# Attention probabilities: the multiply by the reciprocal moves from VectorE to ScalarE in every second head

## The chip, the cores and the metric

The kernel runs on one core of a Trainium2 chip. Its time is the device time of one execution in microseconds (us); before the change it is 2204.34 us, the median of 3 runs (2202.94 to 2204.92). The engines named below are TensorE (PE, with its weight loads PEld), VectorE (DVE), ScalarE (ACT), GpSimd (POOL) and SyncE (SP). Each engine runs its own list of instructions in order and waits at semaphores for the others.

## The reference

One layer of a hybrid encoder for 1024 prompt rows and 64 sample rows: projections, a retention branch with four heads, an attention branch (MLA) with eight heads, gates, an output projection and a SwiGLU stage. The part that matters here is the softmax of the attention:

```python
def mla_attend(q, k_nope, kpe, v, mask):
    scale = (NOPE_DIM + ROPE_DIM) ** -0.5
    s = (jnp.einsum('bqhd,bkhd->bhqk', q[..., :NOPE_DIM], k_nope).astype(jnp.float32)
         + jnp.einsum('bqhr,bkr->bhqk', q[..., NOPE_DIM:], kpe).astype(jnp.float32)) * scale
    s = jnp.where(mask, s, jnp.finfo(jnp.float32).min)
    p = jax.nn.softmax(s, axis=-1)
    return jnp.einsum('bhqk,bkhe->bqhe', p.astype(v.dtype), v)
```

Queries of tile t (128 rows) see keys 0 to 128(t+1); the 64 sample rows see 320 keys.

## The kernel before

The eight attention heads run one after another. A head h has nine tiles in the order 8, 0, 1, ..., 7: tile 8 is the sample rows (64 x 320 scores), tile t has 128 x 128(t+1). A function, `attention_steps(head)`, writes out nine steps per head as a list, and all five engines walk the same list, each doing its own share of every entry. Step k of a head holds, in this order:

- P of tile k+1: the probabilities are normalised. VectorE takes the reciprocal of the row sum (L1875) and multiplies the exponentials `p_exp` in place (L1876); this raises `prob_done`. In a head's last step this is tile 8 of the next head.
- T of tile k: TensorE transposes the probabilities in blocks of up to 512 keys into PSUM (L980, after `prob_done` and after VectorE has emptied the bank); ScalarE copies each block out rounded, `pt_hi` (L1355); VectorE subtracts to get the remainder, `pt_lo` (L1640).
- O of a pair of tiles, in some steps: probabilities times values on TensorE, then `out_hl` high on ScalarE (L1368) and low on VectorE. O also needs a free PSUM bank: the unit two places before it must have been emptied by VectorE (`p_free`).
- D, in the steps after one that made a rotary part: ScalarE copies the rotated query parts to `qr` (L1296, L1297), VectorE subtracts (L1640).
- S of tile k+2: scores on TensorE (L800 to L967), the row maximum on VectorE (L1868, L1869), the exponential with its row sum on ScalarE (L1340).
- F: one to three projection units for the next head, as filling for TensorE: K, Q and V (copied high on ScalarE at L1272, L1283, L1277, low on VectorE). While an odd head (1, 3, 5) runs, three units more belong to the list, R: the rotary query parts of the next two heads. VectorE multiplies these by cosine and sine (L1684 and four pieces of L1675, all on VectorE), GpSimd adds the products (L2206), and D of the next step stores them. In head 7 the filling is the first retention projection, whose inputs are loaded again from DRAM.

`p_exp`, `negmax` and `rowsum` have two buffers each, by the parity of the tile's running number n.

In the texts below the steps of an odd head are called by the P that they begin with: t0 to t7 for its tiles 0 to 7, and "the sample step" for the last step of the even head before it, which holds P of the odd head's tile 8.

Of the kernel before, what the change touches and what calls it, by code (L numbers as in the profile page):

```python
# [8 lines left out]
ACT = mybir.ActivationFunctionType  # L9
AX = mybir.AxisListType  # L10

P = 128
# [124 lines left out]
def keys_of(tile):  # L137

    return (0, (tile + 1) * P, P) if tile < 8 else (SEQ, DEC + PAST, DEC)


def build(nc, a, o):

    with ExitStack() as ctx:
# [5 lines left out]
        def sem(name):  # L150
            return ctx.enter_context(nc.semaphore(name))
# [14 lines left out]
        rowsum = at("rowsum", CON + 1344, [2, 2])  # L166
# [44 lines left out]
        p_exp = [region(f"p_exp{b}", 23.7, [SEQ], extra=4096 * b) for b in range(2)]  # L211
# [131 lines left out]
        max_done = sem("max_done")  # L343
        exp_done = sem("exp_done")
        prob_done = sem("prob_done")
        t_done = sem("t_done")
        t_high = sem("t_high")
        t_low = sem("t_low")
# [68 lines left out]
        def s_index(h, tile):  # L417
            return 9 * h + (0 if tile == 8 else tile + 1)
# [751 lines left out]
        def _(act):  # L1170
# [43 lines left out]
            for t in range(KT):  # L1214
                act.wait_ge(x_in[t], 16)
                nc.scalar.activation(xa_hi[:, t, :], xt[:, t, :], ACT.Copy,
                                     scale=gains[:, G_MIX + t:G_MIX + t + 1]).then_inc(norm_high, 1)
# [106 lines left out]
            for head in range(MH):  # L1324
                for s in attention_steps(head):
                    if s[0] == "F":
                        fill(*s[1:])
                        continue
                    h, tile = s[1:]
                    if s[0] == "D":  # L1330
                        rotary_parts(*s[1:])
                    elif s[0] == "S":
                        n = s_index(h, tile)
                        _, nk, nq = keys_of(tile)
                        act.wait_ge(max_done, n + 1)
                        if n >= 2:
                            act.wait_ge(t_done, t_end(n - 2))
                        bank = 2 * (n % 2)
                        src = ps[0:nq, bank:bank + 2, :].rearrange("p b k -> p (b k)")[:, 0:nk]
                        nc.scalar.activation(p_exp[n % 2][0:nq, 0:nk], src, ACT.Exp,  # L1340
                                             bias=negmax[0:nq, n % 2, 0:1], scale=SCALE,
                                             accum_out=rowsum[0:nq, n % 2, 0:1]).then_inc(exp_done, 1)
                    elif s[0] == "T":
                        _, nk, nq = keys_of(tile)
                        q0 = P * (tile % 2) if tile < 8 else P
                        for i, (k0, nb) in enumerate(t_blocks(tile)):
                            t = t_index(h, tile) + i
                            act.wait_ge(t_done, t + 1)
                            if i == 0 and (tile % 2 == 0) and (h or tile != 8):

                                act.wait_ge(p_done, 1 + (p_order["M", h - 1, "O", 3] if tile == 8 else
                                                     p_order["M", h, "O", tile // 2 - 1 if tile else 4]))
                            full = nb if tile < 8 else 2
                            src = ps[:, 4 + t % 2, 0:full * P].rearrange("p (k q) -> p k q", k=full)[:, :, 0:nq]
                            ins = nc.scalar.activation(pt_hi[:, k0:k0 + full, q0:q0 + nq], src, ACT.Copy)  # L1355
                            if tile == 8:
                                ins = nc.scalar.activation(pt_hi[0:DEC, 2, q0:q0 + nq],
                                                           ps[0:DEC, 4 + t % 2, 2 * P:2 * P + nq], ACT.Copy)
                            ins.then_inc(t_high, 1)
                    elif s[0] == "O":  # L1360
                        pair = s[2]
                        n = o_index(h, pair)
                        w = DEC if pair == 4 else 2 * P
                        u = p_order["M", h, "O", pair]
                        act.wait_ge(p_done, u + 1)
                        if n >= 2:
                            act.wait_ge(o_out[n % 2], 16 * (n // 2))
                        nc.scalar.activation(out_hl[n % 2][:, 0, 0:w], ps[:, 6 + u % 2, 0:w],  # L1368
                                             ACT.Copy).then_inc(p_high, 1)


            for h in range(RH):
                for s in retention_steps(h):
# [4 lines left out]
                    n = 9 * h + c  # L1378
                    L = P if c < 8 else DEC
                    if s[0] == "A":  # L1380
                        col = 1 if c < 8 else 2
                        act.wait_ge(kd_done, n + 1)
                        if n >= 2:
                            act.wait_ge(u_done, n - 1)
                        nc.scalar.activation(kd_f[n % 2][0:L, :], ps[0:L, 3, 0:DK], ACT.Copy,
                                             scale=dcol[0:L, h, col:col + 1]).then_inc(kd_copy, 1)
                    elif s[0] == "B":
                        act.wait_ge(z_done, n + 1)
                        if n >= 2:
                            act.wait_ge(z_norm, n - 1)  # L1390
                        nc.scalar.activation(zs[n % 2][0:L, :], ps[0:L, 1, 0:DV], ACT.Copy,
                                             scale=dcol[0:L, h, 0:1]).then_inc(z_copy, 1)
                    elif s[0] == "Z":
# [3 lines left out]
                        for j in range(2):  # L1397
                            ins = nc.scalar.activation(zt[n % 2][:, j, 0:L], ps[:, 2, j * P:j * P + L], ACT.Copy,
                                                       scale=gains[:, G_GN + 2 * h + j:G_GN + 2 * h + j + 1])
# [69 lines left out]
            for s, t in enumerate(OUT_ORDER):  # L1469
                for g, (c0, c1) in enumerate(GROUPS):  # L1470
                    q = 3 * s + g
                    w = c1 - c0
                    if g == 0:
# [3 lines left out]
                        else:  # L1477
# [3 lines left out]
                                         scale=gains[:, G_F + t:G_F + t + 1]).then_inc(h_gain, 1)  # L1481
# [48 lines left out]
            for pair in range(UP_PAIRS):  # L1530
                n = pair + 1
# [84 lines left out]
        def _(dve):  # L1616
            chained = [0]

            def chain(ins):

                chained[0] += 1
                ins.then_inc(v_chain, 1)
                dve.wait_ge(v_chain, chained[0])
# [227 lines left out]
            for head in range(MH):  # L1851
                for s in attention_steps(head):
                    if s[0] == "F":
                        fill(*s[1:])
                        continue
                    h, tile = s[1:]
                    if s[0] == "D":
                        rotary_parts(*s[1:])
                    elif s[0] == "S":
                        n = s_index(h, tile)  # L1860
                        _, nk, nq = keys_of(tile)
                        bank = 2 * (n % 2)
                        scores = ps[0:nq, bank:bank + 2, :].rearrange("p b k -> p (b k)")
                        dve.wait_ge(s_done, n + 1)
                        if tile < 8:

                            chain(nc.vector.memset(scores[0:64, nk - 64:nk], NEG))
                        chain(nc.vector.reduce_max(negmax[0:nq, n % 2, 1:2], scores[:, 0:nk], AX.X))  # L1868
                        nc.vector.tensor_scalar(negmax[0:nq, n % 2, 0:1], negmax[0:nq, n % 2, 1:2],  # L1869
                                                -SCALE, None, ALU.mult).then_inc(max_done, 1)  # L1870
                    elif s[0] == "P":
                        n = s_index(h, tile)
                        _, nk, nq = keys_of(tile)
                        dve.wait_ge(exp_done, n + 1)
                        chain(nc.vector.reciprocal(rowsum[0:nq, n % 2, 1:2], rowsum[0:nq, n % 2, 0:1]))  # L1875
                        nc.vector.tensor_scalar(p_exp[n % 2][0:nq, 0:nk], p_exp[n % 2][0:nq, 0:nk],  # L1876
                                                rowsum[0:nq, n % 2, 1:2], None, ALU.mult).then_inc(prob_done, 1)
                    elif s[0] == "T":
                        n = s_index(h, tile)
                        _, nk, nq = keys_of(tile)  # L1880
                        q0 = P * (tile % 2) if tile < 8 else P
                        for i, (k0, nb) in enumerate(t_blocks(tile)):
                            t = t_index(h, tile) + i
                            dve.wait_ge(t_high, t + 1)
                            full = nb if tile < 8 else 2
                            src = ps[:, 4 + t % 2, 0:full * P].rearrange("p (k q) -> p k q", k=full)[:, :, 0:nq]
                            ins = low(pt_lo[:, k0:k0 + full, q0:q0 + nq], src, pt_hi[:, k0:k0 + full, q0:q0 + nq])
                            if tile == 8:
                                ins = low(pt_lo[0:DEC, 2, q0:q0 + nq], ps[0:DEC, 4 + t % 2, 2 * P:2 * P + nq],
                                          pt_hi[0:DEC, 2, q0:q0 + nq])  # L1890
                            ins.then_inc(t_low, 1)
                    elif s[0] == "O":
                        pair = s[2]
                        n = o_index(h, pair)
                        w = DEC if pair == 4 else 2 * P
                        u = p_order["M", h, "O", pair]
                        dve.wait_ge(p_high, high_index["M", h, "O", pair] + 1)
                        low(out_hl[n % 2][:, 1, 0:w], ps[:, 6 + u % 2, 0:w],
                            out_hl[n % 2][:, 0, 0:w]).then_inc(p_free, 1)
# [157 lines left out]
            for pair in range(UP_PAIRS):  # L2057
                n = pair + 1
# [387 lines left out]
```

## Time and profile before

| | |
|---|---|
| median of 3 runs | 2204.34 us |
| profiled execution | 2203.62 us, its span 2201.7 us |
| mean granted TensorE clock | 0.972 of full speed |
| busy: PE / PEld / DVE / ACT / POOL | 94% / 90% / 49% / 30% / 16% |
| attention heads | 164 to 582 us of the span |

In the tenths of the span that the page gives (40 slices of 55 us) the attention fills slices 4 to 11, and VectorE shows 7 to 4 tenths there, TensorE 8 and 9:

```profile
PE   7879898987998988999999999988999999999997
DVE  7966767764444433321111224475555556432257
ACT  4434444441112223321121113354434334310010
PEclk9989999998999999999999999999999999999998
```

A line such as `247.68 1.19 DVE L1876 TENSOR_SCALAR p_exp<-p_exp,rowsum 128x896 ... x1` in the trace is: start in the span, duration, engine, line of the kernel, operation, what is written from what, the tile's shape and how many are merged. Square brackets behind it give how long the engine was idle before, and who released it.

### The profile page before, as it was taken

To read this page: it belongs to the slowest core of one execution; us is meant where nothing else is said; L and a number is where in the kernel's file an instruction comes from. 1 tells how busy PE (TensorE), PEld (TensorE's weight loads), DVE (VectorE), ACT (ScalarE), POOL (GpSimd) and SP (SyncE) were. 2 spreads that over 40 slices of the span, in tenths; PEclk is the share of its full clock that TensorE was granted. 3 is DMA by queue.
4 is the path that set the end of the run, shared out by engine and by line. 5 is a ranking of instruction groups with operands and counts; after the bars stand their busy time and mean duration, and the time that the engine had idled before them with its cause. 6 is when DMAs were issued, how large, how long until landed. Compare 5 with 4: busy or idle time off the path is not lost. (4 is left out here: it accounts for less than half of the span.)

```text
span 2201.7 us, 33255 instructions
## 1 busy us (share of the span) xinstructions
PE 2062.5 (94%) x13370; PEld 1979.3 (90%) x13370; DVE 1086.7 (49%) x1820; ACT 662.3 (30%) x1191; POOL 348.9 (16%) x307
## 2 busy tenths in 40 slices
PE   7879898987998988999999999988999999999997
PEld 6768787876998887999999999988999999999997
DVE  7966767764444433321111224475555556432257
ACT  4434444441112223321121113354434334310010
POOL 2110000000122111000000000144444444300000
PEclk9989999998999999999999999999999999999998
DMA  3511110115111112221124112423233232473412
GB/s 146 217 45 41 40 45 31 45 35 212 59 33 59 41 42 72 82 67 42 48 91 158 38 48 79 132 76 119 90 109 115 85 118 98 165 297 137 165 58 82
DMA packets 88842, 201.60 MB, mean 92 GB/s; under 512 B 11664, under 2 KB 42320, under 8 KB 85904
## 3 DMA queue, kind: packets, MB, share of 16 engines
q1 hardware_dynamic: 88720, 199.89, 26.3%
q8 instruction: 86, 1.41, 0.3%
q14 instruction: 36, 0.29, 0.0%
HBM read 141.71 MB, written 58.15 MB: 91 GB/s over the span
## 5 line engine op out<-in xcount | busy, mean ns | idle before, releaser
L800 PE MATMUL ps<-xn_hi,w_hi 128*128 128x384 f32 (+1 forms) x960 | 320.6, 334 | 20.4 <-DMA xn_lo<-xn_spill 12.6
L800 PE MATMUL ps<-sx_hi,t_hi 128*128 128x272 f32 x1056 | 306.3, 290 | 12.1 <-ACT u L1495 5.9
L802 PE MATMUL ps<-xn_lo,w_hi 128*128 128x384 f32 (+1 forms) x960 | 317.5, 331 | 0.0
L801 PE MATMUL ps<-xn_hi,w_lo 128*128 128x384 f32 (+1 forms) x960 | 317.5, 331 | 0.0
L801 PE MATMUL ps<-sx_hi,t_lo 128*128 128x272 f32 x1056 | 306.0, 290 | 0.0
L802 PE MATMUL ps<-sx_lo,t_hi 128*128 128x272 f32 x1056 | 304.8, 289 | 0.0
L800 PEld LDWEIGHTS ps<-sx_hi,t_hi 128*128 128x128 f32 x1056 | 200.8, 190 | 13.1 <-issue 6.9
L800 PEld LDWEIGHTS ps<-xn_hi,w_hi 128*128 128x128 f32 x960 | 183.9, 192 | 24.5 <-DMA xn_lo<-xn_spill 15.7
L801 PEld LDWEIGHTS ps<-sx_hi,t_lo 128*128 128x128 f32 x1056 | 200.5, 190 | 0.1
L802 PEld LDWEIGHTS ps<-sx_lo,t_hi 128*128 128x128 f32 x1056 | 200.5, 190 | 0.0
L801 PEld LDWEIGHTS ps<-xn_hi,w_lo 128*128 128x128 f32 x960 | 183.9, 192 | 0.0
L802 PEld LDWEIGHTS ps<-xn_lo,w_hi 128*128 128x128 f32 x960 | 183.7, 191 | 0.0
L1628 DVE TENSOR_TENSOR w_lo<-w_stage,w_hi 128x1024 fp32r<-128x1024 f32 (+1 forms) x83 | 98.4, 1185 | 121.7 <-ACT w_hi L1177 121.4
L1177 ACT ACTIVATE w_hi<-w_stage 128x1024 fp32r<-128x1024 f32 (+1 forms) x83 | 84.2, 1015 | 156.8 <-PE ps L802 142.9
L800 PE MATMUL ps<-y_hi,w_hi 128*128 128x384 f32 (+1 forms) x384 | 126.3, 329 | 3.8 <-DMA y_lo<-ym_spill 3.8
L802 PE MATMUL ps<-y_lo,w_hi 128*128 128x384 f32 (+1 forms) x384 | 126.2, 329 | 0.0
L801 PE MATMUL ps<-y_hi,w_lo 128*128 128x384 f32 (+1 forms) x384 | 126.1, 328 | 0.0
L2129 DVE TENSOR_TENSOR hacc<-hacc,ps 128x384 f32<-128x384 f32 (+3 forms) x96 | 51.0, 532 | 140.3 <-PE ps L802 140.2
L802 PE MATMUL ps<-yd,dwr_hi 128*128 128x384 f32 (+3 forms) x324 | 105.8, 326 | 0.0
L801 PE MATMUL ps<-yd,dwr_lo 128*128 128x384 f32 (+3 forms) x324 | 105.7, 326 | 0.0
L800 PE MATMUL ps<-yd,dwr_hi 128*128 128x384 f32 (+3 forms) x324 | 105.6, 326 | 0.0
L1340 ACT ACTIVATE p_exp<-ps,negmax 64x320 f32<-64x320 f32 (+8 forms) x72 | 51.7, 718 | 162.2 <-DVE negmax L1869 162.1
(245 smaller groups left out, 4757.3 us busy)
## 6 DMA issues: line engine op xcount, KB each, us to landing
w_stage<-in_weights SPq DMA_DIRECT2D x83, 512.0 KB, 3.7
y_spill<-hg_r SPq DMA_DIRECT2D x44, 544.0 KB, 3.3
yd<-y_spill SPq DMA_DIRECT2D x22, 1088.0 KB, 5.6
raw<-in_weights SPq DMA_DIRECT2D x22, 512.0 KB, 5.1
hg<-in_weights SPq DMA_DIRECT2D x22, 512.0 KB, 5.1
d_stage<-in_weights SPq DMA_DIRECT2D x24, 384.0 KB, 3.1
ym_spill<-out_hl SPq DMA_DIRECT2D x32, 256.0 KB, 2.6
xt<-in_x SPq DMA_DIRECT2D x8, 544.0 KB, 8.1
```

The source lines that it names most:

```text
L800: nc.tensor.matmul(out, wh, xh, start=start, stop=False, skip_group_check=onto)
L801: nc.tensor.matmul(out, wl, xh, start=False, stop=False, skip_group_check=onto)
L802: return nc.tensor.matmul(out, wh, xl, start=False, stop=stop, skip_group_check=onto)
L1177: nc.scalar.activation(w_hi[:, slot, first:8, :], stage[slot][:, first:8, :], ACT.Copy).then_inc(w_high, 1)
L1340: nc.scalar.activation(p_exp[n % 2][0:nq, 0:nk], src, ACT.Exp, bias=negmax[0:nq, n % 2, 0:1], scale=SCALE, accum_out=rowsum[0:nq, n % 2, 0 ...
L1628: nc.vector.tensor_tensor(w_lo[:, slot, first:8, :], stage[slot][:, first:8, :], w_hi[:, slot, first:8, :].bitcast(F32), ALU.subtract).the ...
L2129: nc.vector.tensor_tensor(hacc[:, t, c0:c1], hacc[:, t, c0:c1], ps[:, bank, 0:c1 - c0], ALU.add).then_inc(d_free, 1)
```

## The change

In the heads with an odd number, 36 of the 72 P entries, VectorE only makes the reciprocal and raises a new semaphore, `sum_inv`. ScalarE gets the P entry: it waits for `sum_inv` and multiplies `p_exp` in place with an ACTIVATE whose scale is the per-row reciprocal; it raises `prob_done`. In the even heads nothing changes.

```diff
@@ ScalarE's list
                     elif s[0] == "S":
...
+                    elif s[0] == "P" and h % 2:
+                        n = s_index(h, tile)
+                        _, nk, nq = keys_of(tile)
+                        act.wait_ge(sum_inv, 9 * (h // 2) + n - 9 * h + 1)
+                        nc.scalar.activation(p_exp[n % 2][0:nq, 0:nk], p_exp[n % 2][0:nq, 0:nk], ACT.Copy,
+                                             scale=rowsum[0:nq, n % 2, 1:2]).then_inc(prob_done, 1)
                     elif s[0] == "T":
@@ VectorE's list
                         dve.wait_ge(exp_done, n + 1)
+                        if h % 2:
+                            nc.vector.reciprocal(rowsum[0:nq, n % 2, 1:2], rowsum[0:nq, n % 2, 0:1])\
+                              .then_inc(sum_inv, 1)
+                            continue
                         chain(nc.vector.reciprocal(rowsum[0:nq, n % 2, 1:2], rowsum[0:nq, n % 2, 0:1]))
                         nc.vector.tensor_scalar(p_exp[n % 2][0:nq, 0:nk], p_exp[n % 2][0:nq, 0:nk],
                                                 rowsum[0:nq, n % 2, 1:2], None, ALU.mult).then_inc(prob_done, 1)
```

ScalarE's list in head 1, from the exponential of tile 6 (896 keys) to that of tile 7, before the change (line numbers of the kernel before):

```order
L1340 ACTIVATE p_exp_105,rowsum<-ps,negmax 128x896 [waits t_done,max_done]
L1355 ACTIVATE pt_hi<-ps 128x4x128 [waits t_done]
L1355 ACTIVATE pt_hi<-ps 128x2x128 [waits t_done]
L1296 ACTIVATE qr_111<-tmp_56 64x320 [waits rot_sum]
L1297 ACTIVATE qr_112<-tmp_56 64x320
L1340 ACTIVATE p_exp_106,rowsum<-ps,negmax 128x1024 [waits t_done,max_done]
```

The same place after the change (line numbers of the changed kernel, 1 to 7 higher):

```order
L1341 ACTIVATE p_exp_105,rowsum<-ps,negmax 128x896 [waits t_done,max_done]
L1348 ACTIVATE p_exp_105<-p_exp_105,rowsum 128x896 [waits sum_inv]
L1362 ACTIVATE pt_hi<-ps 128x4x128 [waits t_done]
L1362 ACTIVATE pt_hi<-ps 128x2x128 [waits t_done]
L1297 ACTIVATE qr_111<-tmp_56 64x320 [waits rot_sum]
L1298 ACTIVATE qr_112<-tmp_56 64x320
L1341 ACTIVATE p_exp_106,rowsum<-ps,negmax 128x1024 [waits t_done,max_done]
```

The multiply of tile 6, with its wait for VectorE, now stands ahead of the copies of tile 5's transposed blocks and of the rotary copies.

VectorE's list at the same place, from the last rotation to the next row maximum, before:

```order
L1684 TENSOR_TENSOR tmp_54<-ps,cos_91 128x320 [waits rot_sum,p_done]
L1675 TENSOR_TENSOR tmp_55<-ps,sin_92 32x320 x4
L1875 RECIPROCAL rowsum<-rowsum 128x1 [waits exp_done]
L1876 TENSOR_SCALAR p_exp_105<-p_exp_105,rowsum 128x896 [waits v_chain]
L1640 TENSOR_TENSOR pt_lo<-ps,pt_hi 128x4x128 [waits t_high]
L1640 TENSOR_TENSOR pt_lo<-ps,pt_hi 128x2x128 [waits t_high]
L1640 TENSOR_TENSOR qr_113<-tmp_56,qr_113 64x320 [waits rot_high]
```

And after:

```order
L1883 RECIPROCAL rowsum<-rowsum 128x1 [waits exp_done]
L1647 TENSOR_TENSOR pt_lo<-ps,pt_hi 128x4x128 [waits t_high]
L1647 TENSOR_TENSOR pt_lo<-ps,pt_hi 128x2x128 [waits t_high]
L1647 TENSOR_TENSOR qr_113<-tmp_56,qr_113 64x320 [waits rot_high]
L1647 TENSOR_TENSOR qr_114<-tmp_56,qr_114 64x320
```

The multiply is gone, and what now stands behind the reciprocal waits for a copy that ScalarE makes behind its own multiply.

## Rows read from the trace of the kernel before

**Rows 1.** Two windows: length, busy PE, PEld, DVE, ACT, POOL, granted clock, DMA.

```profile
202.82:257.82 55.00, 48.23 (x308) 42.14 (x306) 41.39 (x95) 21.62 (x55) 3.87 (x5) 1.00 0.13 40
...
340.00:350.00 10.00, 7.28 (x43) 6.71 (x42) 9.12 (x18) 3.29 (x7) 0.86 (x1) 0.85 0.08 26
```

**Rows 2.** Timeline of TensorE: start, duration, operation, idle before it and its releaser.

```profile
205.86 0.36 PE L980 MATMUL ps<-eye,p_exp 64*128 64x64 f32 x3 [0.41 <-DVE pt_lo L1640]
...
222.87 0.36 PE L800 MATMUL ps<-pt_hi,v_hi 128*128 128x256 f32 x1
...
260.86 0.36 PE L980 MATMUL ps<-eye,p_exp 64*128 64x64 f32 x3 [0.80 <-DVE pt_lo L1640]
...
513.57 0.45 PE L800 MATMUL ps<-xn_hi,w_hi 128*128 128x384 f32 x1 [3.62 <-DMA xn_lo<-xn_spill]
```

**Rows 3.** Timeline of VectorE, sample step, then t1 and t2 of head 1.

```profile
204.56 0.15 DVE L1875 RECIPROCAL rowsum<-rowsum 64x1 f32<-64x1 f32 x1
...
205.04 1.27 DVE L1640 TENSOR_TENSOR pt_lo<-ps,pt_hi 128x512 fp32r<-128x512 f32 x2
...
215.22 0.15 DVE L1875 RECIPROCAL rowsum<-rowsum 128x1 f32<-128x1 f32 x1
...
215.68 0.28 DVE L1640 TENSOR_TENSOR pt_lo<-ps,pt_hi 128x128 fp32r<-128x128 f32 x1
...
218.70 0.15 DVE L1875 RECIPROCAL rowsum<-rowsum 128x1 f32<-128x1 f32 x1
...
219.23 0.42 DVE L1640 TENSOR_TENSOR pt_lo<-ps,pt_hi 128x256 fp32r<-128x256 f32 x1
...
221.90 0.56 DVE L1640 TENSOR_TENSOR q_lo<-ps,q_hi 128x384 fp32r<-128x384 f32 x1 [1.23 <-ACT q_hi L1283]
```

**Rows 4.** Timeline of VectorE and GpSimd in t4, t6 and t7 of head 1.

```profile
232.33 0.16 DVE L1875 RECIPROCAL rowsum<-rowsum 128x1 f32<-128x1 f32 x1
...
234.51 1.12 DVE L1640 TENSOR_TENSOR qr<-tmp,qr 64x384 fp32r<-64x384 f32 x2
...
247.48 0.17 DVE L1875 RECIPROCAL rowsum<-rowsum 128x1 f32<-128x1 f32 x1
247.53 0.86 POOL L2206 TENSOR_TENSOR tmp<-tmp,tmp 128x320 f32<-128x320 f32 x1 [6.75 <-DVE tmp L1675]
247.68 1.19 DVE L1876 TENSOR_SCALAR p_exp<-p_exp,rowsum 128x896 f32<-128x896 f32 x1
...
249.95 0.99 DVE L1640 TENSOR_TENSOR qr<-tmp,qr 64x320 fp32r<-64x320 f32 x2
...
254.88 0.15 DVE L1875 RECIPROCAL rowsum<-rowsum 128x1 f32<-128x1 f32 x1
...
255.07 0.75 DVE L1876 TENSOR_SCALAR p_exp<-p_exp,rowsum 128x1024 f32<-128x1024 f32 x1
255.73 1.15 DVE L1640 TENSOR_TENSOR pt_lo<-ps,pt_hi 128x512 fp32r<-128x512 f32 x2
```

**Rows 5.** Timeline of VectorE and ScalarE, between t6 and t7.

```profile
252.36 0.15 DVE L1869 TENSOR_SCALAR negmax<-negmax 128x1 f32<-128x1 f32 x1
252.55 1.11 ACT L1340 ACTIVATE p_exp<-ps,negmax 128x1024 f32<-128x1024 f32 x1 [3.18 <-DVE negmax L1869]
...
253.65 0.59 ACT L1277 ACTIVATE v_hi<-ps 128x512 fp32r<-128x512 f32 x1
254.13 0.98 ACT L1355 ACTIVATE pt_hi<-ps 128x512 fp32r<-128x512 f32 x2
254.27 0.69 DVE L1640 TENSOR_TENSOR v_lo<-ps,v_hi 128x512 fp32r<-128x512 f32 x1 [1.76 <-ACT v_hi L1277]
```

**Rows 6.** Groups by form on ScalarE: count, then busy us and mean ns.

```profile
L1340 ACT ACTIVATE p_exp<-ps,negmax 128x512 f32<-128x512 f32 x8 | 5.5, 689 | 17.9 <-DVE negmax L1869 17.9
...
L1296 ACT ACTIVATE qr<-tmp 64x384 fp32r<-64x384 f32 x6 | 3.2, 526 | 14.5 <-POOL tmp L2206 14.5
...
L1216 ACT ACTIVATE xa_hi<-xt,gains 128x1088 fp32r<-128x1088 f32 x8 | 9.6, 1202 | 1.5 <-DMA xt<-in_x 1.2
```

More of the change, by code:

```diff
@@ L345, in build @@
         prob_done = sem("prob_done")
+        sum_inv = sem("sum_inv")
         t_done = sem("t_done")
```

## The prediction

> **What bounds the kernel now.** I read the page first: TensorE is busy 94% of the span, so only a place where TensorE waits can carry a change on another engine. Then the windows, a row per head: in the 55.00 us of head 1 TensorE is busy 48.23, so it waits 6.8 us, although VectorE, at 41.39 us, has room on average [rows 1]. Then the timelines of TensorE and VectorE side by side. TensorE waits at the joint of heads 0 and 1 for `pt_lo` (0.41 us) and again at the joint of 1 and 2 (0.80 us) [rows 2]. Traced back from the second joint, VectorE runs without a gap from the first rotation to the row maximum before t7, and from there VectorE and ScalarE take turns: maximum, exponential, `v_hi`, `v_lo`, reciprocal, multiply, `pt_lo`, maximum. The reader is to see the turns in [rows 5]: ScalarE starts 0.04 us after VectorE's 252.51 end, VectorE 0.03 us after ScalarE's 254.24, and neither does anything else useful in between. From the sample step to the first rotation (some 24 us) TensorE sets the pace. So VectorE's chain is the path from the first rotation of an odd head to the start of the next head, and in the sample step. Heads 1, 3 and 5 have this pattern; head 7 has not.
>
> **What the change does in one step.** Before: reciprocal, multiply, `pt_lo` at once, because ScalarE had copied `pt_hi` meanwhile. After: reciprocal; 0.04 us to ScalarE; the multiply there, A; the copy of the first block of `pt_hi`, H, which starts 0.10 us before A's end (254.13 against 253.65 + 0.59 [rows 5]); 0.03 us back. From the start of the reciprocal to `pt_lo` that is 0.15 + 0.04 + A - 0.10 + H + 0.03 = A + H + 0.12. ScalarE is free when the reciprocal comes, since its exponential is long done.
>
> Prices. H: the 512-wide copy of PSUM takes 0.59 us [rows 5]. The slope of ScalarE is (1.11 - 0.689) / 512, 0.053 us per 64 elements [rows 5, 6]; so H is 0.38 at 256 wide and 0.27 at 128. A is not in the trace; the nearest row has the same shape of operation, SBUF to SBUF with a per-row scale: 1.202 us at 1088 elements [rows 6]. By the slope A is 1.15 at 1024, 1.04 at 896, 0.83 at 640, 0.62 at 384, 0.57 at 320, 0.52 at 256. It could be as low as an exponential without its pointer, some 0.1 less each, or as high as one without the 0.10 overlap; I take the row, and keep both ends.
>
> **Step by step**, new interval less old:
>
> - Sample step (320 wide, 512-wide block): 0.57 + 0.59 + 0.12 = 1.28 against 0.48 (204.56 to 205.04 [rows 3]): +0.80. TensorE waits for this `pt_lo` already [rows 2], so all of it counts.
> - t0: `pt_lo` waits for TensorE, not for the multiply: nothing.
> - t1: 0.52 + 0.27 + 0.12 = 0.91 against 0.46: +0.45. t2: 0.62 + 0.38 + 0.12 = 1.12 against 0.53: +0.59 [rows 3]. TensorE sets the pace here and needs neither `pt_lo` at once. But both delay the exponential behind which ScalarE copies `q_hi`, and so `q_lo`, which ended at 222.46 [rows 3], by 0.80 + 0.45 + 0.59 = 1.84, to 224.30. O of the first pair needs the bank that `q_lo` frees. It began at 222.87 [rows 2]; now 224.30 + 0.06 for the hand-over. So TensorE is 1.49 late there, not 0.80: a new wait of 0.69 us. t3 is absorbed: VectorE waits for TensorE's scores behind it.
> - t4, t5, t6, the rotary steps, with VectorE on the path: here `pt_lo` itself is hardly later (the multiply it loses took 1.19 us at 896 wide [rows 4]), but the copies of the rotary part stand behind on ScalarE. t4, reciprocal to `qr` low: 0.16 + 0.04 + 0.83 - 0.10 + 0.49 (a 512-wide block less the overlap) + 2 x 0.53 + 0.03 = 2.51 against 2.18 (232.33 to 234.51): +0.33. t6: 0.16 + 0.04 + 1.04 - 0.10 + 0.77 (0.49 and 0.28, two blocks) + 2 x 0.47 + 0.03 = 2.88 against 2.47: +0.41 [rows 4, 6]. (The second `qr` size by the same slope.) t5 lies between, 0.37. Together +1.11.
> - t7: 1.15 + 0.59 + 0.12 = 1.86 against 0.85 (254.88 to 255.73 [rows 4]): +1.01. Its cover, that ScalarE copies early, is gone, and the turns of VectorE and ScalarE are the path.
> - The last P of an odd head belongs to an even head: unchanged. In the even head every engine starts later by the same amount, and TensorE sets the pace, so nothing is won back.
>
> An odd head costs 1.49 + 1.11 + 1.01 = 3.61 us with its sample step. Three of them: 10.8. Head 7 adds only its sample step, 0.80: this delays the last O of head 6, whose emptied bank lets the input loads start, and TensorE then waits for these (3.62 us at 513.57 [rows 2]). Behind them its steps are long retention projections without waits, so P of head 7 is hidden. Sum: +11.6 us. The profiled execution took 2203.62 us; 2203.62 + 11.6 = 2215.2. The median of the runs is 0.72 above the profiled one: 2216.
>
> Behind the attention TensorE works almost without waits, so I let the delay pass to the end undiminished.
>
> **Two rules weighed.** In t6 the multiply on VectorE took 1.19 us for 896 elements while GpSimd added (247.53 to 248.39); in t7, where GpSimd does nothing, 0.75 for 1024 [rows 4]. The Trainium skill, "SBUF — State Buffer", section "Who interferes with whom", has it that VectorE and GpSimd share a port pair that one holds for a whole instruction, and that ScalarE has its own. The trace agrees; by that rule alone the move would pay in t4 to t6. Against it stands the Trainium skill, "ScalarE: Activation LUTs", section "Rules for kernel authors", which wants a plain multiply on VectorE; and its section on the table load gives 186 ns plus 0.833 ns per element plus 93 ns for a pointer, an estimate of 1.13 us at 1024, with which the sum would be some 0.4 us less. No run so far shows this very instruction.
>
> **Rivals.**
>
> 1. *Covered multiply, faster.* Place: t4 to t7. VectorE loses 1.19 us three times and 0.75 once per odd head, 4.3 us, and if ScalarE's copies did not follow its multiply, VectorE would be early by this: 3 x 4.3 = 13 us, 2204.3 - 13 = 2191. For it: VectorE really is without a gap there. Against: the order of ScalarE's list. It decides from A + H + 0.12 below the old interval; in t6 A would have to be about 0.7 instead of 1.04 for `pt_lo`, and lower for `qr`. 7 in 100.
> 2. *Hidden, no change.* The waits at the joints would have to have room; they are all put down to VectorE. Within 0.2%, 2200 to 2208.8: 6 in 100.
> 3. *No wait at the O bank.* If `q_lo` does not hold it, a head costs 0.80 + 1.11 + 1.01 = 2.92; 3 x 2.92 + 0.80 = +9.6, 2214. With the low end of A besides, 0.4 to 0.5 less per head: +8, 2212. 20 in 100 for up to 2213.
> 4. *The clock.* In head 3, with the gaps of TensorE as in head 1, the granted clock fell to 0.85 in 10 us, part of it at 1.2 instead of 2.4 GHz [rows 1]; there it cost nearly nothing, since VectorE was the path. Wider gaps could bring it in each odd head and where TensorE is the path: 10 x 0.15 = 1.5 us each, +4.5 on my sum, 2220. 10 in 100.
>
> **Numbers.** My own case, 2213 to 2218.5 (the high end is 0.10 without overlap in seven steps of each head, +2.1), has 57 in 100. The range goes from 2209 to 2220: it leaves out the first two rivals and the far end of the fourth. 0.2%, 4.4 us, is about what a measurement of this kernel can tell from no change. Faster 0.07, same 0.06, slower 0.87.
>
> **What would show it.** Right: in the odd heads ScalarE's new line takes 0.83 us at 640 and 1.15 at 1024; VectorE has a new idle time before `pt_lo`, released by `pt_hi`, of some 1 to 1.5 us in t1 to t7; TensorE has a new wait of about 0.7 us before O of the first pair; the joints of the heads move: 205.86 to 260.86, 55.0 us, becomes 57.8, and the even head after it is 0.8 us longer by its sample step, and behind 582 us nothing moves. Wrong: if VectorE's maxima of t5 to t7 come earlier than before relative to the joint, the first rival holds; if the joints are as far apart as before, the second.

## The result and the profile after

The changed kernel takes 2215.52 us, the median of 4 runs (2214.13 to 2218.94), against 2203.72 us for the kernel before (4 runs, 2202.94 to 2204.92): ratio 1.0055, 95% interval 1.0038 to 1.0073, slower by 11.8 us. 2216 was predicted. The single executions scatter by several us (4.8 us among the four of the changed kernel), so that the median fell within 0.5 us of the forecast is partly luck; what follows goes by the profiled pair. The profiled execution took 2214.64 us against 2203.62, +11.02, with a span of 2212.7; its mean granted clock is 0.972 as before.

The page's busy line of the changed kernel: VectorE gives up 24 us (1086.7 before), ScalarE takes 24 (662.3 before), TensorE's share falls since the span grows.

```profile
PE 2061.9 (93%) x13370; PEld 1979.2 (89%) x13370; DVE 1062.9 (48%) x1784; ACT 686.2 (31%) x1227; POOL 348.1 (16%) x307
```

The timeline of TensorE, changed kernel, at the places of [rows 2]. A "joint" here is the start of the three merged transposes of a head's sample tile, where one head ends and the next begins. First the joint of heads 0 and 1, then O of the first pair, then the transposes of tile 6, then the joint of heads 1 and 2:

```profile
206.89 0.36 PE L981 MATMUL ps<-eye,p_exp 64*128 64x64 f32 x3 [1.19 <-DVE pt_lo L1647]
...
224.61 0.36 PE L801 MATMUL ps<-pt_hi,v_hi 128*128 128x256 f32 x1 [0.49 <-issue]
...
252.37 1.72 PE L981 MATMUL ps<-eye,p_exp 128*128 128x128 f32 x7 [3.18 <-DVE pt_lo L1647]
...
264.55 0.36 PE L981 MATMUL ps<-eye,p_exp 64*128 64x64 f32 x3 [1.17 <-DVE pt_lo L1647]
```

ScalarE's exponential ahead of the first of these joints, kernel before, then changed kernel:

```profile
202.82 0.52 ACT L1340 ACTIVATE p_exp<-ps,negmax 64x320 f32<-64x320 f32 x1 [1.47 <-DVE negmax L1869]
```

```profile
203.07 0.52 ACT L1341 ACTIVATE p_exp<-ps,negmax 64x320 f32<-64x320 f32 x1 [1.47 <-DVE negmax L1876]
```

This execution was already 0.25 us late at the exponential ahead of the joint (203.07 against 202.82). The wait at the first joint grew from 0.41 to 1.19 us, by 0.78. O has a new wait, for which the trace names no releaser (`issue`); the next timeline shows whom it fits. From joint to joint head 1 takes 264.55 - 206.89 = 57.66 us instead of 55.00, and head 2, to the joint at 307.20, 42.65 instead of 41.80.

The timeline of VectorE, changed kernel, in the sample step, t1, t2, t4, t6 and t7, answers to [rows 3] and [rows 4]:

```profile
204.80 0.14 DVE L1883 RECIPROCAL rowsum<-rowsum 64x1 f32<-64x1 f32 x1
206.06 1.29 DVE L1647 TENSOR_TENSOR pt_lo<-ps,pt_hi 128x512 fp32r<-128x512 f32 x2 [1.11 <-ACT pt_hi L1362]
...
217.13 0.29 DVE L1647 TENSOR_TENSOR pt_lo<-ps,pt_hi 128x128 fp32r<-128x128 f32 x1 [0.74 <-ACT pt_hi L1362]
...
221.27 0.42 DVE L1647 TENSOR_TENSOR pt_lo<-ps,pt_hi 128x256 fp32r<-128x256 f32 x1 [0.95 <-ACT pt_hi L1362]
...
223.95 1.02 DVE L1647 TENSOR_TENSOR q_lo<-ps,q_hi 128x384 fp32r<-128x384 f32 x2 [1.23 <-ACT q_hi L1284]
...
234.06 0.16 DVE L1883 RECIPROCAL rowsum<-rowsum 128x1 f32<-128x1 f32 x1
...
236.55 1.12 DVE L1647 TENSOR_TENSOR qr<-tmp,qr 64x384 fp32r<-64x384 f32 x2 [0.25 <-ACT qr L1298]
...
249.78 0.16 DVE L1883 RECIPROCAL rowsum<-rowsum 128x1 f32<-128x1 f32 x1
251.53 1.02 DVE L1647 TENSOR_TENSOR pt_lo<-ps,pt_hi 128x512 fp32r<-128x512 f32 x2 [1.59 <-ACT pt_hi L1362]
252.64 0.98 DVE L1647 TENSOR_TENSOR qr<-tmp,qr 64x320 fp32r<-64x320 f32 x2
...
257.56 0.15 DVE L1883 RECIPROCAL rowsum<-rowsum 128x1 f32<-128x1 f32 x1
259.41 1.16 DVE L1647 TENSOR_TENSOR pt_lo<-ps,pt_hi 128x512 fp32r<-128x512 f32 x2 [1.70 <-ACT pt_hi L1362]
```

In every step shown `pt_lo` has a wait that it did not have before, 0.74 us in t1 to 1.70 in t7, and its releaser is `pt_hi`. The `q_lo` at 223.95 is two merged blocks; the first of them, at the 0.56 us that one takes in [rows 3], ends at 224.51, and O starts 0.10 us behind it, at 224.61. Ahead of `pt_hi` stands ScalarE's own new instruction; groups by form, changed kernel, of the attention:

```profile
L1348 ACT ACTIVATE p_exp<-p_exp,rowsum 128x1024 f32<-128x1024 f32 x4 | 4.6, 1150 | 6.6 <-DVE rowsum L1883 6.6
...
L1348 ACT ACTIVATE p_exp<-p_exp,rowsum 128x640 f32<-128x640 f32 x4 | 3.3, 833 | 15.4 <-DVE rowsum L1883 15.4
```

### The profile page after: what moved, and what is told of

Read it like the earlier page. It is cut to its first block and busy times, and to the rows that moved or that the text cites. A ratio compares the mean times of both kernels' runs of the same rounds, so it can differ in the third digit from the quotient of the medians.

```text
span 2212.7 us, 33255 instructions
## 1 busy us (share of the span) xinstructions
PE 2061.9 (93%) x13370; PEld 1979.2 (89%) x13370; DVE 1062.9 (48%) x1784; ACT 686.2 (31%) x1227; POOL 348.1 (16%) x307
## 5 line engine op out<-in xcount | busy, mean ns | idle before, releaser
L801 PEld LDWEIGHTS ps<-sx_hi,t_hi 128*128 128x128 f32 x1056 | 200.8, 190 | 13.1 <-issue 6.9
```

Of the source, the lines that this page charges most:

```text
L801: nc.tensor.matmul(out, wh, xh, start=start, stop=False, skip_group_check=onto)
```

## The experiments

Single medians turned out to scatter by more than some effects here, so the parts are read by the joints, which stand once per head in TensorE's timeline. Before, head 1 takes 55.00 us from joint to joint [rows 2], head 2 41.80, head 3 55.16 and head 5 55.00.

**Four parts of the change.** Each moves only some of the multiplies; `moved` is the list of their running numbers.

```diff
-                    elif s[0] == "P" and h % 2:
+                    elif s[0] == "P" and on_act(h, tile):
...
-                        act.wait_ge(sum_inv, 9 * (h // 2) + n - 9 * h + 1)
+                        act.wait_ge(sum_inv, moved.index(n) + 1)
...
-                        if h % 2:
+                        if on_act(h, tile):
```

with `on_act` true in odd heads for tile 8 (part_sample), tiles 0 to 3 (part_t0_t3), 4 to 6 (part_t4_t6), or 7 (part_t7).

> Only the sample tile's multiply (320 keys) of heads 1, 3, 5 and 7 goes to ScalarE, 4 of the 36 moved ones; the rest stays on VectorE. Theory (the multiply stands in series ahead of the pt_hi copy that VectorE waits for): the joint ahead of each odd head comes 0.78 us later and TensorE's wait there grows from 0.41 to about 1.2 us; three heads and head 7: +3.1 us in all; inside the odd head nothing moves (205.9 to 260.9 stays 55.0 us). Rival by busy time (the cost follows the time that ScalarE gains): 4 x 0.56 of the 26 us moved, so 9% of 11 us, +1 us. Rival that only the rotary steps count: 0.

> Only the multiplies of tiles 0 to 3 in the odd heads go to ScalarE, 16 of 36. Theory: VectorE is 0.45 + 0.59 = 1.04 us later at q_lo of the first Q unit, and O of the first pair waits for the bank that it frees: 0.7 us more per head of 1, 3 and 5, seen as a new idle time of TensorE of some 0.5 us or more before O, and nothing behind it; +2.1 us in all. Rival by busy time: 16 x 0.56 of 26 us, +3.8 us. Rival (TensorE sets the pace here, all is hidden): 0.

> Only the multiplies of tiles 4 to 6 in the odd heads go to ScalarE, 12 of 36. Theory: the multiply that VectorE loses is as long as what it waits for, but the qr copies stand behind: +0.31, +0.27, +0.39 us from reciprocal to the low part of qr, 0.97 per head of 1, 3 and 5, so +2.9 us; in head 7 nothing. Rival by busy time: 12 x 0.94 of 26 us, +4.8 us. Rival that the freed VectorE time (1.2 us each) is worth something here when nothing else is changed: below 0.

> Only the multiply of tile 7 (1024 keys) in the odd heads goes to ScalarE, 4 of 36. Theory: reciprocal to pt_lo goes from 0.85 to 1.85 us, all of it on the path at the end of heads 1, 3 and 5: +3.0 us; in head 7 nothing. Rival by busy time: 4 x 1.15 of 26 us, +1.9 us. Rival that TensorE hides it: 0.

The first and the last line of each fence are the two joints of head 1 in TensorE's timeline; in part_t0_t3 the O stands between them. part_sample:

```profile
206.76 0.36 PE L986 MATMUL ps<-eye,p_exp 64*128 64x64 f32 x3 [1.19 <-DVE pt_lo L1652]
...
261.74 0.36 PE L986 MATMUL ps<-eye,p_exp 64*128 64x64 f32 x3 [0.80 <-DVE pt_lo L1652]
```

part_t0_t3:

```profile
207.86 0.36 PE L986 MATMUL ps<-eye,p_exp 64*128 64x64 f32 x3 [0.41 <-DVE pt_lo L1652]
225.59 0.35 PE L806 MATMUL ps<-pt_hi,v_hi 128*128 128x256 f32 x1 [0.50 <-issue]
...
263.58 0.36 PE L986 MATMUL ps<-eye,p_exp 64*128 64x64 f32 x3 [0.79 <-DVE pt_lo L1652]
```

part_t4_t6:

```profile
207.32 0.36 PE L986 MATMUL ps<-eye,p_exp 64*128 64x64 f32 x3 [0.40 <-DVE pt_lo L1652]
...
263.25 0.36 PE L986 MATMUL ps<-eye,p_exp 64*128 64x64 f32 x3 [0.79 <-DVE pt_lo L1652]
```

part_t7:

```profile
207.88 0.36 PE L986 MATMUL ps<-eye,p_exp 64*128 64x64 f32 x3 [0.40 <-DVE pt_lo L1652]
...
263.86 0.36 PE L986 MATMUL ps<-eye,p_exp 64*128 64x64 f32 x3 [1.16 <-DVE pt_lo L1652]
```

| kernel | time in us, ratio to before (95%) | head 1, joint to joint | more | expected |
|---|---|---|---|---|
| part_sample | 2207.35, 1.0016 (1.0005 to 1.0028) | 54.98 | 0; the wait ahead of it +0.78 | 0; +0.78 |
| part_t0_t3 | 2207.99, 1.0017 (1.0005 to 1.0028) | 55.72 | +0.72 | +0.7 |
| part_t4_t6 | 2207.51, 1.0014 (1.0002 to 1.0025) | 55.93 | +0.93 | +0.97 |
| part_t7 | 2208.68, 1.0018 (1.0006 to 1.0029) | 55.98 | +0.98 | +1.0 |
| the change | 2215.52, 1.0055 (1.0038 to 1.0073) | 57.66 | +2.66 | +2.8 |

The three inner parts sum to 2.63 us, the whole gives 2.66: they are independent links of one path. By the rival of busy time the four would have been 1, 3.8, 4.8 and 1.9 us; by the joints they are 4 x 0.78 = 3.1, 3 x 0.72 = 2.2, 3 x 0.93 = 2.8 and 3 x 0.98 = 2.9, together 11.0. The medians alone would not decide this: the four parts are 2.7, 3.4, 2.9 and 4.1 us above the kernel before as measured beside them (2204.62), together 13.1, each with an interval of some 2.5 us to either side. The waits stand where each part says: 1.19 us at the joint for the sample, 0.50 at O for t0 to t3, 1.16 at the far joint for t7. No rival that hides one of them is left.

**The place in the list: late_odd, late_all.** The multiply on ScalarE moves behind the copies of the transposed blocks: in late_odd the multiplies of the odd heads, as in the change, in late_all those of all heads but the very first tile. ScalarE's list, against the kernel before; `scaled_late` is the wait and the ACTIVATE of the change.

```diff
+                    elif s[0] == "P" and on_act(h, tile):
+                        pending = (h, tile)
...
                             ins.then_inc(t_high, 1)
+                        if pending is not None:
+                            scaled_late(*pending)
+                            pending = None
```

> As the changed kernel, but in ScalarE's list the multiply of tile k+1 stands behind the copies of tile k's transposed blocks (pt_hi), so VectorE goes from the reciprocal straight to pt_lo. Theory (the loss came from the place in the list, the series of multiply and copy): reciprocal to pt_lo shrinks to some 0.15 to 0.2 us, the joints ahead of the odd heads come 0.4 us earlier than in the kernel before; in t4 nothing is won (the qr low part waits for GpSimd's sum and the two qr copies, 0.05 + 1.01 + 0.04 + 1.06 + 0.03 us from the end of the rotation, as late as before), t5 wins 0.55, t6 0.3, t7 0.7: 1.9 us per odd head with its sample step, and 0.4 for head 7: 6 us faster than the kernel before, some 2197.5, and 17 faster than the changed kernel. Rival (ScalarE's multiply itself costs, wherever it stands, since prob_done comes later): same as the changed kernel, +11. Rival (all of the multiply's time on VectorE is won): 13 us faster than before.

> As late_odd, but for all heads (71 of the 72 multiplies; only the very first stays on VectorE). Theory: in the even heads TensorE sets the pace but for the joint behind an odd head, where TensorE waited 0.80 us for pt_lo; that comes 0.35 us earlier for three heads: 1 us more than late_odd, 2196.5. Rival (VectorE's busy share is what matters): twice the gain of late_odd, 2191.

late_odd: 2203.44 us, ratio 0.9996 (0.9987 to 1.0005), not to be told from before, and 12 us below the change. The series of multiply and copy was thus the whole cost; the rival that ScalarE's multiply costs wherever it stands fell. But 6 us of gain had been forecast, and by the medians 1 came. Part of the rest was lost in the attention and part behind it. In the attention: timeline of VectorE and ScalarE, late_odd, t7 of head 1:

```profile
253.74 0.15 DVE L1896 RECIPROCAL rowsum<-rowsum 128x1 f32<-128x1 f32 x1
253.81 1.13 DVE L1660 TENSOR_TENSOR pt_lo<-ps,pt_hi 128x512 fp32r<-128x512 f32 x2
253.93 1.15 ACT L1335 ACTIVATE p_exp<-p_exp,rowsum 128x1024 f32<-128x1024 f32 x1
254.98 0.36 ACT L1388 ACTIVATE out_hl<-ps 128x256 fp32r<-128x256 f32 x1
255.38 0.42 DVE L1660 TENSOR_TENSOR out_hl<-ps,out_hl 128x256 fp32r<-128x256 f32 x1 [0.43 <-ACT out_hl L1388]
```

`pt_lo` is 0.07 us behind the reciprocal, as forecast (0.85 before), but `out_hl`'s copy now stands behind the multiply and takes back 0.43. And TensorE was granted less clock: timeline of TensorE, late_odd, the V unit behind this, and the window around it.

```profile
253.97 2.97 PE L897 MATMUL ps<-w_full,ckn 128*128 128x128 f32 x16 [2.12 <-DVE v_lo L1660]
```

```profile
250.00:260.00 10.00, 7.88 (x53) 7.45 (x52) 6.46 (x15) 6.30 (x12) 0.00 (x0) 0.83 0.08 26
```

The columns are length, busy PE, PEld, DVE, ACT, POOL, granted clock and DMA, as in [rows 1]. The same unit takes 2.02 us in head 5 of this run, behind the same wait of 2.12 us; here part of it ran at 1.2 GHz, and the next joint, for which TensorE waited for nobody this time, came no earlier: 205.24 to 260.51, 55.27 us. Head 3 has the same (55.24), head 5, where the window 440 to 450 shows the clock at 1.00, 54.20: 0.8 us won. From the first joint (165.64) to the last (494.20) the run is still 2.5 us shorter than the kernel before (165.86 to 496.89). It lost that later, in a stage that the edit does not touch. Two VectorE instructions of the retention stage and the window from 700 to 900 us, before:

```profile
598.82 0.56 DVE L1684 TENSOR_TENSOR tmp<-ps,cos 128x384 f32<-128x384 f32 x1 [3.48 <-PE ps L802]
...
901.58 0.56 DVE L1940 TENSOR_TENSOR tmp<-tmp,tmp 128x384 f32<-128x384 f32 x1 [1.60 <-ACT tmp L1409]
```

```profile
700.00:900.00 200.00, 178.02 (x1110) 165.08 (x1109) 78.24 (x189) 56.95 (x131) 30.13 (x57) 0.94 0.19 57
```

The same two instructions and the window, late_odd:

```profile
596.04 0.56 DVE L1704 TENSOR_TENSOR tmp<-ps,cos 128x384 f32<-128x384 f32 x1 [3.48 <-PE ps L808]
...
901.18 0.56 DVE L1964 TENSOR_TENSOR tmp<-tmp,tmp 128x384 f32<-128x384 f32 x1 [1.60 <-ACT tmp L1429]
```

```profile
700.00:900.00 200.00, 180.06 (x1101) 166.42 (x1102) 75.94 (x185) 55.39 (x128) 29.76 (x57) 0.92 0.19 57
```

The lead of 2.8 us at the first place is 0.4 us at the second, and the granted clock from 700 to 900 us is 0.92 instead of 0.94; TensorE is busy 2 us longer there for nine matmuls fewer. Over the whole span the eleven runs of late_odd have 0.967 to 0.972, the 27 of the kernel before that were measured beside them 0.971 to 0.974. Why a kernel that differs in the attention gets less clock there is not shown.

late_all: 2204.52 us, 1.0001 (0.9992 to 1.0010). It too is shorter than before between its first and last joint, by 1.8 us, and its heads 3 and 5 take 53.8 us. At the joints ahead of the odd heads TensorE now waits 0.60 to 0.62 us for ScalarE's multiply itself, which is too late for the transposes, where it waited 0.40 to 0.42 for `pt_lo` before. Both expectations on late_all missed.

**The kernel before with another order on VectorE: dve_swap.** For tiles 4 to 6 of the odd heads, reciprocal and multiply stay on VectorE but stand behind `pt_lo`.

```diff
+                    elif s[0] == "P" and h % 2 and 4 <= tile <= 6:
+                        pending = (h, tile)
...
                             ins.then_inc(t_low, 1)
+                        if pending is not None:
+                            normalised(*pending)
+                            pending = None
```

> The kernel before, all multiplies on VectorE, but for tiles 4 to 6 of the odd heads reciprocal and multiply stand behind pt_lo in VectorE's list, away from GpSimd's sum. Theory (the 1.2 us multiply of these steps is two things at once, 0.55 to 0.69 us of work and the rest a block by GpSimd's sum): it takes 0.55 at 640, 0.62 at 768 and 0.69 at 896 where GpSimd has ended, t4 wins nothing (bound by the qr copies), t5 and t6 0.5 us each: 3 us faster than before, 2201. Rival (the multiply is slow for its own size or the place in PSUM traffic): still 1.2 us and no gain.

2199.84 us, ratio 0.9981 (0.9972 to 0.9990): faster by 4 to 5 us. Head 1 takes 53.86 us from joint to joint, 1.14 less, so 3 x 1.14 = 3.4 us by the joints. VectorE's timeline, dve_swap, the multiply of t6, against 1.19 us in [rows 4]:

```profile
247.54 0.69 DVE L1856 TENSOR_SCALAR p_exp<-p_exp,rowsum 128x896 f32<-128x896 f32 x1
```

**GpSimd's sum behind the multiply: pool_behind.** The same question from the other side: VectorE's list as before, but GpSimd waits.

```diff
                 if NG < r < ROT_MLA:
                     pool.wait_ge(rot_low, r)
+                if 2 * NG <= r < ROT_MLA:
+                    pool.wait_ge(prob_done, s_index(2 * (r // NG) - 3, 4 + r % NG) + 1)
```

> The kernel before, but GpSimd's sum of the rotary products in t4, t5 and t6 of heads 1, 3 and 5 waits until VectorE has multiplied (on prob_done). Theory (VectorE's multiply is blocked while GpSimd's sum runs; and the qr low part hangs on that sum and two qr copies): the multiplies take 0.55, 0.62 and 0.69 us instead of 1.21, 1.28 and 1.19; but the chain sum, qr, qr now starts behind them, so the qr low parts come 0.76, 0.26 and 0.34 us later than before: 1.36 us per head, +4 us. Rival (the multiply is slow there by itself): it stays at 1.2 us and the loss is 3 x (1.25 + 1.0) us or more. Rival (what VectorE is freed of is won): 1.9 us per head faster, -5.6 us.

Timeline of VectorE and GpSimd, pool_behind, t6:

```profile
248.26 0.17 DVE L1875 RECIPROCAL rowsum<-rowsum 128x1 f32<-128x1 f32 x1
248.46 0.69 DVE L1876 TENSOR_SCALAR p_exp<-p_exp,rowsum 128x896 f32<-128x896 f32 x1
249.18 1.02 DVE L1640 TENSOR_TENSOR pt_lo<-ps,pt_hi 128x512 fp32r<-128x512 f32 x2
249.32 0.86 POOL L2208 TENSOR_TENSOR tmp<-tmp,tmp 128x320 f32<-128x320 f32 x1 [7.18 <-DVE p_exp L1876]
...
251.19 0.99 DVE L1640 TENSOR_TENSOR qr<-tmp,qr 64x320 fp32r<-64x320 f32 x2 [0.99 <-ACT qr L1297]
```

The multiply took 0.55, 0.62 and 0.69 us at 640, 768 and 896 elements, as expected, at its old place in VectorE's list: what made it 0.50 to 0.66 us longer before was GpSimd's sum beside it. And VectorE waits 0.99 us for the `qr` copies: sum, copy, copy is a chain of its own. The time is 2211.69 us, 1.0035 (1.0023 to 1.0046), +8 where +4 was expected. VectorE's t6 is 1.7 us late relative to the first joint (251.19 - 205.43 against 249.95 - 205.86) where 1.36 was expected. From there to the next joint head 1 (57.45 us in all) takes another 0.8 us more than before (262.88 - 251.19 against 260.86 - 249.95), and the granted clock is 0.83 in the window 256 to 266; that the one made the other is argued, not shown. The odd heads together account for the profiled pair: the last joint is 503.28 - 496.89 = 6.4 us late, the end of the span 6.0. The median of the six runs lies 2.2 us above this profiled one (2209.46), which no trace here explains.

**A version that is faster: swap_sample, swap_both.** dve_swap, and on ScalarE only those multiplies for which nobody was expected to wait: the odd heads' sample tile, and in swap_both tile 7 too. They stand behind its copies of `pt_hi` and, where an O follows, of `out_hl`.

```diff
+                    elif s[0] == "P" and on_act(h, tile):
+                        pending = (h, tile)
...
                             ins.then_inc(t_high, 1)
+                        if pending is not None and not o_follows(h, tile):
+                            scaled_late(*pending)
+                            pending = None
...
                                              ACT.Copy).then_inc(p_high, 1)
+                        if pending is not None:
+                            scaled_late(*pending)
+                            pending = None
```

> The swap of tiles 4 to 6 on VectorE (multiply behind pt_lo, as in dve_swap), and besides the sample tile's multiply of the odd heads on ScalarE, but behind its copies of pt_hi, where nobody waits for it. Theory: the joints ahead of heads 1, 3, 5 and 7 come 0.38 us earlier each: 1.5 us less than dve_swap, 4.9 to 5.5 us below the kernel before. Rival (a multiply on ScalarE costs wherever it stands): 1 to 3 us more than dve_swap.

> As swap_sample, and tile 7's multiply too on ScalarE, behind the copies of pt_hi and of out_hl. Theory: reciprocal to pt_lo in t7 goes from 0.85 to 0.07 us with out_hl not delayed; the maximum of the next head's sample tile comes 0.75 us earlier; but T of tile 7 waits for the multiply on ScalarE, ready at about the time at which it now starts, so TensorE takes the path for part of it: 0.5 us per head more than swap_sample, 7 us below the kernel before. Rival (the clock falls at the joint, as in two heads of late_odd, where 16 small matmuls took 2.97 and 3.64 us instead of 2.02): no gain over swap_sample, or 1 to 2 us lost.

swap_sample: 2200.79 us, 0.9985 (0.9976 to 0.9994), by the median no better than dve_swap. By the joints what was expected came: they stand 0.52, 0.42, 0.15 and 0.44 us nearer to the joint before them than in dve_swap, 1.5 us together; the smallest is head 5's, where TensorE waits 0.26 us for ScalarE's multiply instead of 0.40 for `pt_lo`. But this profiled execution reached head 0's joint at 168.27 us, dve_swap's at 165.43, ahead of everything that the edits touch, and one trace of each cannot say how much of the difference of the medians comes from there (see the last section). swap_both: 2196.66 us, 0.9966 (0.9954 to 0.9978), faster than the kernel before by 7.3 us where 7 was expected, and than the change by some 19; between its first and last joint it is also 7.3 us shorter than before (323.71 against 331.03). Timeline of VectorE and ScalarE, swap_both, t7 of head 1:

```profile
252.51 0.15 DVE L1910 RECIPROCAL rowsum<-rowsum 128x1 f32<-128x1 f32 x1
252.58 1.14 DVE L1666 TENSOR_TENSOR pt_lo<-ps,pt_hi 128x512 fp32r<-128x512 f32 x2
252.61 0.41 ACT L1391 ACTIVATE out_hl<-ps 128x256 fp32r<-128x256 f32 x1
252.87 1.18 ACT L1338 ACTIVATE p_exp<-p_exp,rowsum 128x1024 f32<-128x1024 f32 x1
253.63 0.42 DVE L1666 TENSOR_TENSOR out_hl<-ps,out_hl 128x256 fp32r<-128x256 f32 x1
```

With the copies ahead, the same ScalarE instruction (1.18 us here, 1.15 in the change) makes nobody wait: TensorE enters the next joint without a wait, and head 1 takes 257.69 - 204.61 = 53.08 us.

## Why the prediction was right

Its steps against the changed kernel's profile, head 1:

- *Price of the multiply, A.* Taken from a row of another line at 1088 elements with the exponential's slope. 0.83 at 640, 1.15 at 1024 came out: 0.833 and 1.150 measured. From the figures of the Trainium skill, "ScalarE: Activation LUTs", section "What ACT_TABLE_LOAD costs", the estimate for 1024 is 1.13 us; the row was nearer.
- *Sample step* +0.80: 206.06 - 204.80 = 1.26 against 0.48, +0.78, all of it in TensorE's wait. part_sample shows it alone.
- *t1, t2, and O's bank*: O at 224.61, 1.49 later than before less the 0.25 that this execution was late: 224.61 - 222.87 - 0.25 = 1.49, as forecast. The idle time itself is 0.49 us and not the 0.7 named as its sign, because the profile counts it from the modelled end of the transposes ahead of it; O's start, relative to the joint, is 0.71 later. That the bank freed by `q_lo` is what it waits for rests on the times (0.10 us behind the block's end), since the trace names no releaser. This was the step with the least support, since no row of before showed the wait; part_t0_t3 shows it alone, with 0.72 us.
- *t4 and t6* +0.33 and +0.41: 2.49 and 2.86 measured where 2.51 and 2.88 stood, +0.31 and +0.39. t5 was set between them at 0.37; it is 0.27.
- *t7* +1.01: 1.85 against 0.85, +1.00.
- *New idle time of VectorE before `pt_lo`*: "some 1 to 1.5 us" was said; it is 0.74 (t1) to 1.70 (t7).
- *The even heads give nothing back*: 42.65 against 41.80, of which 0.78 is the sample step of the next head.
- *P of head 7 is hidden*: not quite as told. TensorE waits there 1.48 us for ScalarE's multiply of one tile (0.99 for VectorE's before) and 0.18 for `pt_lo`; this goes into the wait for the input loads behind it, which for the first two units is 1.58 and 2.97 us instead of 3.62 and 1.92.
- *Head 7 and behind.* At the last joint the kernel is 508.20 - 496.89 = 11.3 us late, 0.25 of them from ahead of the first joint, at the end of the span 11.0. So the joints give 11.1 where the sum had 11.6: t5 is 0.1 less per head, and the sample step, t4 and t6 0.02 each.

The rivals. *Covered multiply* needed ScalarE's copies done before its multiply; late_odd has this, and swap_both for two of the tiles, and the change has not. Even then its 13 us are not to be had, since in t4 to t6 the `qr` chain from GpSimd's sum, which the rival did not look at, holds VectorE: in late_odd it waits 1.29 us for the `qr` copies in t4 and 0.90 in t6, and its t4 has `qr` 4.47 us behind the start of the rotation's sine part, exactly as before. *Hidden* fell with the joints. *No wait at the O bank* fell with part_t0_t3. *The clock* stayed out of the changed kernel's time: 0.972 over the span as before, and its heads 1, 3 and 5 take 57.66, 57.65 and 57.64 us, although the granted clock was 0.83 in the windows 250 to 260 and 450 to 460 and 1.00 in all of head 3. It did cost late_odd its gain in two heads.

The rule weighed in the prediction: dve_swap and pool_behind free the multiply of GpSimd's sum, and it takes 0.55 to 0.69 us instead of 1.19 to 1.28. The Trainium skill, "SBUF — State Buffer", section "Who interferes with whom", has VectorE and GpSimd share a pair of ports; these runs agree with it.

The median moved by 11.8 us, the profiled pair by 11.0; the interval, 8.4 to 16 us, holds both.

## What to carry to other kernels

When work moves to an engine with spare time, look at what stands behind it in that engine's list and who waits for that: the price here was the multiply plus the copy behind it, in series, less what the old engine had spent, and the same instruction behind the copies cost nothing or nearly so. Sum the new interval link by link only on the stretches where the engine is the path, and look at freed buffers as well as at data. Read small effects by a landmark that recurs in the trace; whole-run medians blurred 0.7 us per head, and a clock that came out lower in a later stage hid a gain of 2.5 us.

## What the runs showed of the hardware

- A VectorE multiply of fp32 from SBUF to SBUF takes 0.69 us at 896 elements alone and 1.19 with a GpSimd sum of 0.86 us beside it; at 640 it is 0.55 and 1.21, at 768 0.62 and 1.28. As far as the profile places GpSimd's work, the extra time is the overlap less 0.2 us in all four cases at hand: 0.66 for 0.86, 0.66 for 0.85 and 0.50 for 0.71 before the change, and 0.07 for 0.28 at 640 in dve_swap, where the multiply starts late in the sum. A ScalarE multiply of the same tile beside the same sum takes its usual 1.04.
- An ACTIVATE with a per-row scale in SBUF takes 1.150 us at 1024 elements and 0.403 at 128, and the next one starts 0.1 us before its end.
- Ahead of the attention all kernels here are the same, and still their profiled executions start it at different times, 165.07 to 168.27 us. In the window 20 to 30 us the granted clock is 1.00 in six of the twelve traces, with the first attention transposes at 165.07 to 165.94 us, and 0.83 in the other six, with five of them at 167.29 to 168.27 and one, the changed kernel's, at 166.10. The rows below are part_sample's and part_t7's, whose transposes come at 165.94 and 167.90 us. That the one follows from the other is argued, not shown, and the changed kernel speaks against it as the whole reason.

```profile
20.00:30.00 10.00, 8.20 (x47) 7.62 (x48) 9.89 (x7) 1.24 (x2) 2.25 (x1) 1.00 0.21 70
```

```profile
20.00:30.00 10.00, 8.23 (x38) 7.97 (x39) 9.89 (x7) 0.65 (x2) 2.33 (x1) 0.83 0.16 62
```
